# Value blocks of three attention stages one round earlier, and a projection slab in two drains

## The chip, the cores and the metric

The kernel runs on one core of a Trainium2 chip. It is written by hand, one instruction stream for each engine: TensorE (PE) for matmuls and transposes, VectorE (DVE), ScalarE (ACT), GpSimd (POOL) and SyncE (SP), which issues the loads. The engines meet only at semaphores. The metric is the device time of one execution in microseconds, as the median of some runs.

## The reference

Two blocks of a language model run one after the other on one sequence of 512 tokens with 1024 channels; all arrays are float32. The first is one layer, the second has two, so there are three attention stages, each with an input projection, an output projection and a feed-forward part.

```python
# first block: compressed, windowed and selected attention, 8 heads each, width 64
o_nsa = gates[..., 0:1] * o_cmp + gates[..., 1:2] * o_slc + gates[..., 2:3] * o_win
mixed = jnp.concatenate([o_nsa, o_swa], axis=-1) @ w_out
h = h + rms_norm(mixed, attn_post_norm)
# second block, layer 0: 8 heads of softmax attention, 8 of stick-breaking attention
o = jnp.concatenate([merge_heads(mla), merge_heads(sb)], axis=-1)
return o @ w_o
# second block, layer 1: 16 heads of softmax attention with a decay
return merge_heads(o) @ w_o
# both: x = x + mixer(norm(x)); x = x + ffn(norm(x))
```

In stick-breaking attention the weights are products of sigmoids along the keys, not a softmax.

## The kernel before

**Arithmetic.** A projection is done in three matmuls of a fast format (`mm3`, L853 to L855) on high and low halves of both operands. GpSimd splits each weight slab (128 x 1024) into `w_hi` and `w_lo` (`split_slab`, L462); the four slab rooms and the two rooms of `raw` are handed back through the semaphores `slab_used` and `split`. An output projection has two groups (c = 0 and 1, each 512 columns) of four slabs (s); a slab is four tiles (t), one for each 128 tokens, of six matmuls each, and each tile has its own PSUM bank. Slab s needs channels 256 s to 256 s + 255 of the attention's result, that is two pairs of heads, as halves `xt_hi` and `xt_lo`.

**Attention by rounds.** The stages `first` (12 pairs of heads), `mix` (8 pairs, the last 4 stick-breaking) and `fox` (8 pairs) are run by one scheme, class `Pairs` (L527). A step g is one pair and one block of 128 queries, the longest first: g modulo 4 = 0, 1, 2, 3 has 4, 3, 2, 1 blocks of keys (of `first`, the first four pairs have two at most). Every engine walks through the same rounds r in program order:

- TensorE (`pe_pair_attend`, L1215): the scores of step r; then the value blocks that `value_blocks(r)` lists (`values`, L1255, matmuls at L1266, into bank 6); then it turns the probabilities of step r-2 with transposes (L1239) into banks 4 and 5, in some rounds with the inverses of a pair's sums (L1251); then what the stage's hooks add.
- VectorE (`dve_pair_attend`, L2381): the maxima of step r, or for stick-breaking the scan along the keys (`products`, L2404); copies of the turned probabilities into `p_turn` (L2426) and of the inverses into `inv_t` (L2433); `scaled` (L2448), which reads bank 6 and multiplies by the inverses; for stick-breaking `low` (L2458).
- ScalarE (`act_pair_attend`, L1857): the exponentials (L1868) or sigmoids (L1872), its part of the copies (L1879, L1881, L1888), `high` (L1896), and hooks.
- GpSimd (`pool_first`, `pool_pairs`): widens the inverses (L674), splits the first slabs of the coming projection in the middle of the stage, and splits a pair's result into halves (`halves`, L676).

The scores go round among five banks (in `first` up to step 31 among four); those of a step wait until the exponentials of earlier steps on the same banks are done. Banks 4 and 5 hold one step's turned probabilities, so the next turning waits for both copies of the one before. Bank 6 holds one pair's output: `values` with block 0 waits until `scaled` or `low` of the pair before has read it.

**When.** For pair p the value blocks stood in rounds 4p+8 (block 0), 4p+9 (1) and 4p+10 (2 and 3), for the last pair all in 4p+8. `scaled` came in round 4p+11 (the last pair 4p+9), as did `high` and `low` of stick-breaking, and GpSimd's and ScalarE's work on a pair is placed by `scaled_round` too. After the last scores a stage has eight to ten further rounds, its drain; then comes the output projection (`pe_out_direct`, L1083, for `mix` and `fox`), slab by slab. The drain of `first` already holds two slabs of its projection by hooks (L1443 to L1446). `first` also finishes the input projection's last turnings in hooks of its early rounds; one of them, `window_there`, waits for a copy out of bank 6.

## Time and profile before

| | us |
|---|---|
| median of three runs | 1941.33 |
| lowest and highest of them | 1937.68, 1943.10 |
| the profiled execution's own time | 1936.56 |
| its span, first to last instruction | 1934.8 |
| mean granted clock of TensorE | 0.994 |
| attention of `first` | about 131 to 285 |
| attention of `mix`, its projection | about 797 to 884.5, to 928 |
| attention of `fox`, its projection | about 1444 to 1524.7, to 1568 |

The profile page gives each engine's busy time and the chain of work that ended last. The other views are windows (busy time of each engine in a stretch, with the granted clock as a share of 2.4 GHz), waits (for whom an engine stood still, in total, how often, the longest) and instructions in order of time. Busy time of matmuls overlaps with the next matmul's start, so a single duration is longer than the step from one to the next.

### The profile page before, as it was taken

The numbers are of one execution on the slowest core, as the hardware profiler recorded it, in microseconds if no ns is written. First come the engines' busy times: TensorE is split into PE (matmuls) and PEld (weight loads), VectorE is DVE, ScalarE is ACT, GpSimd is POOL, SyncE is SP. The second block draws the span as 40 slices with busy tenths as digits, with TensorE's granted clock in tenths as the row PEclk, the third lists the DMA queues.
The fourth block names the chain that finished last, engine by engine and source line by source line (L and its number), as shares of the span: only waits on it lengthen the run. The fifth ranks groups of instructions, "written<-read, shape, count | busy, mean of one in ns | idle before, by whom it ended". The sixth has DMA issues, their size and how long they took to land.

```text
span 1934.8 us, 28081 instructions
## 1 busy us (share of the span) xinstructions
PE 1865.5 (96%) x10416; PEld 1500.4 (78%) x10416; DVE 807.2 (42%) x1286; ACT 469.6 (24%) x1145; POOL 1081.9 (56%) x713
## 2 busy tenths in 40 slices
PE   8989899999999999989999999999998999999999
PEld 7776578888888887747888888887875688888887
DVE  4646756765670146671323321114527333223200
ACT  2136533222220144462211110112326221111100
POOL 6754244766666555233566666656534456666663
PEclk9999999999999999999999999999999999999999
DMA  4330022323333232201233332323211123323332
GB/s 158 105 96 13 2 77 66 105 91 98 108 98 98 74 95 69 66 23 55 88 98 96 93 95 91 104 67 98 88 55 45 32 89 98 93 93 97 98 98 87
DMA packets 122557, 159.50 MB, mean 82 GB/s; under 512 B 8546, under 2 KB 83810, under 8 KB 122465
## 3 DMA queue, kind: packets, MB, share of 16 engines
q1 hardware_dynamic: 122465, 158.21, 26.6%
q8 instruction: 65, 1.06, 0.2%
q14 instruction: 27, 0.22, 0.0%
HBM read 155.04 MB, written 2.10 MB: 81 GB/s over the span
## 4 chain that ended last, share of the span: by engine, by line
PE 89%; DVE 6%; ACT 3%; issue 1%; DMA 0%; SPq 0%; DVEq 0%; ACTq 0%
PE ps L853 25%; PE ps L855 25%; PE ps L854 25%; PE ps L1266 3%; PE ps L1239 2%; PE ps L863 1%; DVE p_turn L2426 1%; PE ps L1314 1%; PE ps L1330 1%; DVE gains L2506 1%; PE ps L1041 1%; ACT dump L1613 1%; PE ps L1344 1%; ACT tok L1868 0%; DMA h<-in_x 0%
## 5 line engine op out<-in xcount | busy, mean ns | idle before, releaser
L471 POOL TENSOR_TENSOR w_lo<-raw,w_hi 128x1024 fp32r<-128x1024 f32 (+1 forms) x256 | 605.4, 2365 | 21.4
L469 POOL TENSOR_SCALAR w_hi<-raw 128x1024 fp32r<-128x1024 f32 (+1 forms) x256 | 270.1, 1055 | 502.2 <-PE ps L855 470.6
L853 PE MATMUL ps<-xt_hi,w_hi 128*128 128x512 f32 (+2 forms) x1096 | 420.3, 383 | 0.9 <-ACT tok L2042 0.9
L855 PE MATMUL ps<-xt_hi,w_lo 128*128 128x512 f32 (+2 forms) x1096 | 419.7, 383 | 0.0
L854 PE MATMUL ps<-xt_lo,w_hi 128*128 128x512 f32 (+2 forms) x1096 | 419.6, 383 | 0.0
L853 PE MATMUL ps<-w_hi,xt_hi 128*128 128x512 f32 (+3 forms) x672 | 258.9, 385 | 8.2 <-DVE tok L2541 4.5
L855 PE MATMUL ps<-w_hi,xt_lo 128*128 128x512 f32 (+3 forms) x672 | 254.8, 379 | 0.0
L854 PE MATMUL ps<-w_lo,xt_hi 128*128 128x512 f32 (+3 forms) x672 | 254.8, 379 | 0.0
L2227 DVE TENSOR_TENSOR ps<-ps,gains 128x512 f32<-128x512 f32 x132 | 92.1, 698 | 373.6 <-PE ps L855 373.6
L853 PEld LDWEIGHTS ps<-xt_hi,w_hi 128*128 128x128 f32 (+1 forms) x1096 | 205.2, 187 | 42.3 <-POOL w_lo L485 1.3
L854 PEld LDWEIGHTS ps<-xt_lo,w_hi 128*128 128x128 f32 (+1 forms) x1096 | 205.2, 187 | 40.9
L855 PEld LDWEIGHTS ps<-xt_hi,w_lo 128*128 128x128 f32 (+1 forms) x1096 | 205.2, 187 | 40.9
L853 PE MATMUL ps<-w_hi,hid_hi 128*128 128x512 f32 x528 | 205.6, 389 | 0.0
L855 PE MATMUL ps<-w_hi,hid_lo 128*128 128x512 f32 x528 | 205.4, 389 | 0.0
L854 PE MATMUL ps<-w_lo,hid_hi 128*128 128x512 f32 x528 | 205.4, 389 | 0.0
L853 PEld LDWEIGHTS ps<-w_hi,xt_hi 128*128 128x128 f32 x672 | 127.0, 189 | 34.8 <-issue 6.0
L855 PEld LDWEIGHTS ps<-w_hi,xt_lo 128*128 128x128 f32 x672 | 126.8, 189 | 23.3
L854 PEld LDWEIGHTS ps<-w_lo,xt_hi 128*128 128x128 f32 x672 | 127.1, 189 | 21.5
L2154 DVE TENSOR_TENSOR h<-ps,h 128x512 f32<-128x512 f32 x32 | 22.0, 692 | 253.6 <-PE ps L855 253.6
L853 PEld LDWEIGHTS ps<-w_hi,hid_hi 128*128 128x128 f32 x528 | 99.1, 188 | 20.6
L854 PEld LDWEIGHTS ps<-w_lo,hid_hi 128*128 128x128 f32 x528 | 99.1, 188 | 20.6
L855 PEld LDWEIGHTS ps<-w_hi,hid_lo 128*128 128x128 f32 x528 | 99.1, 188 | 20.5
(324 smaller groups left out, 2195.7 us busy)
## 6 DMA issues: line engine op xcount, KB each, us to landing
raw<-in_w_up SPq DMA_DIRECT2D x88, 256.0 KB
raw<-in_l_w_gate SPq DMA_DIRECT2D x88, 256.0 KB
raw<-in_l_w_up SPq DMA_DIRECT2D x88, 256.0 KB
raw<-in_l_w_down SPq DMA_DIRECT2D x40, 512.0 KB
raw<-in_l_w_in SPq DMA_DIRECT2D x36, 512.0 KB
raw<-in_w_down SPq DMA_DIRECT2D x20, 512.0 KB
raw<-in_l_w_o SPq DMA_DIRECT2D x16, 512.0 KB
raw<-in_w_in SPq DMA_DIRECT2D x12, 512.0 KB
```

Source lines behind the costliest of these rows:

```text
L469: e.tensor_scalar(w_hi[:, s, 0:width], r, 1.0, 0.0, ALU.mult, ALU.add).then_inc(split, 1)
L471: e.tensor_tensor(w_lo[:, s, 0:width], r, w_hi[:, s, 0:width].bitcast(F32), ALU.subtract).then_inc(split, 1)
L853: e.matmul(o, s_hi, m_hi, start=start, stop=False)
L854: e.matmul(o, s_hi, m_lo, start=False, stop=False)
L855: return e.matmul(o, s_lo, m_hi, start=False, stop=stop)
L863: m = e.transpose(bank(turn_bank(name, i), P, t * P, w), staged(name, c)[:, t, off:off + w], ident[:, :])
L1041: m = e.transpose(bank(BY_COLUMNS[name][k], P, t * P), h[:, t, k * P:(k + 1) * P], ident[:, :])
L1239: m = e.transpose(bank(4 + y, HD, (2 * kb + x) * HD), st.prob(g, x)[r, kb * P:(kb + 1) * P], ident[r, r])
L1266: m = e.matmul(ps[x * HD:(x + 1) * HD, 6 * W + kb * P:6 * W + (kb + n) * P], value(p, x, kb), st.rooms["p_turn"][:, p % 2, x, 4 * kb:4 * k ...
L1314: e.matmul(bank(b[x], n), qp[r, q, i * P:(i + 1) * P], kk[r, k, k0 * P:(i + 1) * P], start=True, stop=False)
L2154: e.tensor_tensor(h[:, t, cs], out_half(name, c, t), h[:, t, cs], ALU.add).then_inc(*od.done(*at(f"{name}_res", NT * c + t + 1)))
L2227: e.tensor_tensor(b, b, rs_rows, ALU.mult).then_inc(*od.done(*at(f"{name}_r", 4 * gi + (j + 1))))
```

## The change

Value blocks, `scaled`, and `high` and `low` of stick-breaking stand in earlier rounds: block 0 in 4p+7, block 1 in 4p+8, blocks 2 and 3 in 4p+9, `scaled`, `high` and `low` in 4p+9; the last pair has all of its in 4p+7. A new `split_round` holds the old round numbers for GpSimd's and ScalarE's work behind `scaled`, so that its place in their orders stays. The hook `window_there` goes from round 7 to round 6. And the tiles of slab 0 of group 0 of the second and third output projection are issued by hooks in the drain: tile 0 behind round 32, tile 1 behind 33, tiles 2 and 3 behind 34, each with waits for the exponentials that used its bank; `pe_out_direct` begins with slab 1.

```diff
--- before.py
+++ after.py
@@ -549,7 +549,10 @@
             return band_prob_at(g, x) if g < 4 * self.banded else prob_at(g, x)
 
         def scaled_round(self, p):
-            return max(self.values_round(p) + 1, self.inverse_round(p) + 1)
+            return max(self.values_round(p), self.inverse_round(p))
+
+        def split_round(self, p):
+            return 4 * p + (11 if p < self.pairs - 1 else 9)
 
         def is_soft(self, g):
             return g < 4 * self.soft
@@ -565,16 +568,16 @@
             out = []
             for p in range(self.pairs):
                 if p == self.pairs - 1:
-                    rounds = {4 * p + 8: (0, 2, 1, 3) if p < self.banded else (0, 1, 2, 3)}
+                    rounds = {4 * p + 7: (0, 2, 1, 3) if p < self.banded else (0, 1, 2, 3)}
                 elif p < self.banded:
-                    rounds = {4 * p + 8: (0, 2), 4 * p + 9: (1,), 4 * p + 10: (3,)}
+                    rounds = {4 * p + 7: (0, 2), 4 * p + 8: (1,), 4 * p + 9: (3,)}
                 else:
-                    rounds = {4 * p + 8: (0,), 4 * p + 9: (1,), 4 * p + 10: (2, 3)}
+                    rounds = {4 * p + 7: (0,), 4 * p + 8: (1,), 4 * p + 9: (2, 3)}
                 out += [(p, kb) for kb in rounds.get(r, ())]
             return out
 
         def values_round(self, p):
-            return 4 * p + (8 if p == self.pairs - 1 else 10)
+            return 4 * p + (7 if p == self.pairs - 1 else 9)
 
         def inverse_round(self, p):
             return self.turn_round(4 * p + 7) if p + 1 < self.pairs else 4 * p + 6
@@ -657,9 +660,9 @@
             if r in slabs:
                 split_slab(e, *slabs[r], SLAB)
             for p in range(12):
-                if 4 <= p < 11 and r == first.scaled_round(p) + 1:
+                if 4 <= p < 11 and r == first.split_round(p) + 1:
                     added(p)
-                if ends(p) and r == first.scaled_round(p) + (1 if p < 4 or p == 11 else 2):
+                if ends(p) and r == first.split_round(p) + (1 if p < 4 or p == 11 else 2):
                     squared(p)
 
     def pool_pairs(e, st, slabs, steps=None, value_step=None):
@@ -690,7 +693,7 @@
             if steps and r in steps:
                 value_step(steps[r])
             for p in range(st.soft):
-                if r == st.scaled_round(p) + 1:
+                if r == st.split_round(p) + 1:
                     halves(p)
 
     @block.gpsimd
@@ -1080,16 +1083,32 @@
                     if norm and s - s0 == 2:
                         pe_turn_pair(e, norm, 0)
 
+    def out_tile(e, name, there, c, s, t):
+
+        if t == 0:
+            e.wait_ge(split, 2 * (4 * (phases[name].g0 + c) + s) + 2)
+            if c == 0:
+                e.wait_ge(*there[s])
+        m = slab_tile(e, name, c, s, OUT_KTS[s], x_model, KD - 1, t)
+        if t == 3:
+            m.then_inc(slab_used, 1)
+
+    def out_drain(e, name, there, probs, last):
+
+        def first_tiles(a, b, p):
+            e.wait_ge(*at(probs, p))
+            for t in range(a, b):
+                out_tile(e, name, there, 0, 0, t)
+
+        return {last + 1: lambda: first_tiles(0, 1, 2 * last), last + 2: lambda: first_tiles(1, 2, 2 * last),
+                last + 3: lambda: first_tiles(2, 4, 2 * last + 2)}
+
     def pe_out_direct(e, name, there, norm):
 
         for c in range(2):
             for s in range(4):
-                e.wait_ge(split, 2 * (4 * (phases[name].g0 + c) + s) + 2)
-                if c == 0:
-                    e.wait_ge(*there[s])
-                for t in range(NT):
-                    m = slab_tile(e, name, c, s, OUT_KTS[s], x_model, KD - 1, t)
-                m.then_inc(slab_used, 1)
+                for t in range(NT) if c or s else ():
+                    out_tile(e, name, there, c, s, t)
                 if c == 1 and s == 1:
                     pe_turn_columns(e, norm, 0)
 
@@ -1430,9 +1449,8 @@
 
         def scores_second():
             scores(1)
-            window_there()
-
-        hooks = {1: banks_there, 3: window_first, 5: scores_first, 7: scores_second, 11: lambda: turned(0),
+
+        hooks = {1: banks_there, 3: window_first, 5: scores_first, 6: window_there, 7: scores_second, 11: lambda: turned(0),
                  13: lambda: turned(1)}
         for k in range(4):
             hooks[15 + 2 * k] = lambda k=k: values(k)
@@ -1546,11 +1564,12 @@
                    lambda c: [at("in2_copy", 4 * c + 4)]
                    + ([at("in2_tok", 4 if c == CQ else 4 * HEAD_CHUNKS[c] + 8)] if c == CQ or c in HEAD_CHUNKS else []),
                    "n5")
+        mixed_halves = [at("mix_lo", 2), at("mix_lo", 4), at("mix_slo", 2), at("mix_slo", 4)]
         heads_of = lambda v: lambda p, x, kb: v[:, kb, (2 * p + x) * HD:(2 * p + x + 1) * HD]
         pe_pair_attend(e, mix, mix_scores, heads_of(v2), [at("in2_tpa", 6), at("in2_tpd", 9), at("in2_copy", 31)],
-                       [at("in2_copy", 32), at("in2_tpa", 12), at("in2_tpd", 15)])
-        pe_out_direct(e, "out2", [at("mix_lo", 2), at("mix_lo", 4), at("mix_slo", 2), at("mix_slo", 4)],
-                      "n6")
+                       [at("in2_copy", 32), at("in2_tpa", 12), at("in2_tpd", 15)],
+                       out_drain(e, "out2", mixed_halves, "mix_p", mix.steps - 1))
+        pe_out_direct(e, "out2", mixed_halves, "n6")
         pe_up(e, "up2", "n6")
         pe_down(e, "down2", "up2", "n7")
 
@@ -1589,10 +1608,11 @@
                    lambda c: ([at("in3_copy", 4 * wide("in3", c) + 4), at("in3_tok", 4 * FOX_CHUNKS[c] + 4)]
                               if c in FOX_CHUNKS else []),
                    "n7", {(2, 0): turn_logits, (2, 1): decays, (2, 2): turn_decays, (2, 3): turn_first})
+        fox_halves = [at("fox_lo", 2 * s + 2) for s in range(4)]
         pe_pair_attend(e, fox, fox_scores, heads_of(v3),
                        [at("in3_tpa", 8), at("in3_tpd", 8), at("picks", 6), at("fox_ck", 1)],
-                       [at("in3_copy", 24)])
-        pe_out_direct(e, "out3", [at("fox_lo", 2 * s + 2) for s in range(4)], "n8")
+                       [at("in3_copy", 24)], out_drain(e, "out3", fox_halves, "fox_p", fox.steps - 1))
+        pe_out_direct(e, "out3", fox_halves, "n8")
         pe_up(e, "up3", "n8")
         pe_down(e, "down3", "up3", None)
 
@@ -1820,7 +1840,7 @@
         for k in range(4):
             hooks[16 + 2 * k] = [lambda e, od, k=k: outputs(e, od, k)]
         for p in ENDS:
-            r = first.scaled_round(p) + (1 if p < 4 or p == 11 else 2)
+            r = first.split_round(p) + (1 if p < 4 or p == 11 else 2)
             hooks.setdefault(r, []).append(lambda e, od, p=p: high(e, od, p))
         return layer, hooks
 
@@ -1909,7 +1929,7 @@
             for hook in hooks.get(r, ()) if hooks else ():
                 hook(e, od)
             for p in range(st.soft, st.pairs):
-                if r == st.values_round(p) + 1:
+                if r == st.values_round(p):
                     high(p)
         if st.soft < st.pairs:
             e.preload_act_table_set(EXP_LN)
@@ -2328,7 +2348,7 @@
                  11: [lambda e, od: weights(e, od, 1)], 29: [lambda e, od: variance(e, od, 0)],
                  31: [lambda e, od: dve_refine(e, od, "first", 1, NT, 16)]}
         for p in ENDS:
-            hooks.setdefault(first.scaled_round(p) + (2 if p < 4 or p == 11 else 3), []).append(
+            hooks.setdefault(first.split_round(p) + (2 if p < 4 or p == 11 else 3), []).append(
                 lambda e, od, p=p: low(e, od, p))
         return hooks, variance
 
@@ -2472,7 +2492,7 @@
                 if r == st.scaled_round(p):
                     scaled(p)
             for p in range(st.soft, st.pairs):
-                if r == st.values_round(p) + 1:
+                if r == st.values_round(p):
                     low(p)
             for hook in hooks.get(r, ()) if hooks else ():
                 hook(e, od)
```

## Rows read from the trace of the kernel before

**Rows 1.** The page: busy time of the engines, and the chain that ended last.

```profile
PE 1865.5 (96%) x10416; PEld 1500.4 (78%) x10416; DVE 807.2 (42%) x1286; ACT 469.6 (24%) x1145; POOL 1081.9 (56%) x713
...
PE 89%; DVE 6%; ACT 3%; issue 1%; DMA 0%; SPq 0%; DVEq 0%; ACTq 0%
```

**Rows 2.** Windows: span, then busy us of PE, PEld, DVE, ACT, POOL, clock, DMA.

```profile
130.00:285.00 155.00, 138.87 (x1463) 95.02 (x1463) 104.50 (x219) 81.13 (x278) 52.76 (x46) 0.98 0.09 27
...
834.10:884.50 50.40, 37.65 (x421) 20.92 (x417) 33.39 (x48) 28.57 (x76) 7.21 (x8) 0.97 0.04 12
884.50:906.30 21.80, 21.80 (x98) 18.05 (x97) 2.77 (x4) 3.64 (x7) 10.31 (x6) 1.00 0.16 49
```

**Rows 3.** Waits of PE, 1444 to 1535: us in total, times, longest.

```profile
PE ps L1266 <- DVE o_sb L2448: 5.8, 7, 1.8
PE ps L1239 <- DVE p_turn L2426: 2.9, 7, 0.5
```

**Rows 4.** Waits of PE, 130 to 285.

```profile
PE ps L1239 <- DVE p_turn L2426: 3.6, 8, 0.8
PE ps L1266 <- DVE gains L2448: 3.5, 5, 0.9
...
PE ps L1239 <- ACT p_turn L1879: 1.0, 2, 0.5
...
PE ps L1266 <- DVE mixed L2448: 0.4, 1, 0.4
```

**Rows 5.** Waits of PE, 797 to 885.

```profile
PE ps L1266 <- DVE xt_lo L2458: 5.0, 3, 2.3
PE ps L1239 <- ACT p_turn L1881: 3.5, 4, 0.9
PE ps L1239 <- DVE p_turn L2426: 1.9, 1, 1.9
PE ps L1239 <- DVE inv_t L2433: 1.5, 1, 1.5
```

**Rows 6.** PE in order of time, 1505 to 1525: start, us, instructions, [idle before].

```profile
1505.24 1.08 PE L1266 MATMUL ps<-p_turn,v 128*64 128x512 f32 x4 [0.56 <-DVE o_sb L2448]
...
1511.99 0.28 PE L1239 MATMUL ps<-ident,tok 64*128 64x64 f32 x2 [0.39 <-DVE p_turn L2426]
...
1514.38 1.97 PE L1266 MATMUL ps<-p_turn,v 128*64 128x512 f32 x4 [1.80 <-DVE o_sb L2448]
...
1522.37 2.38 PE L1266 MATMUL ps<-p_turn,v 128*64 128x512 f32 x16 [1.21 <-DVE o_sb L2448]
1524.67 0.50 PE L853 MATMUL ps<-w_hi,xt_hi 128*128 128x512 f32 x1
```

**Rows 7.** Windows behind two waits of PE.

```profile
1514.38:1520.70 6.32, 6.32 (x37) 2.59 (x38) 1.38 (x4) 0.55 (x2) 2.44 (x3) 0.50 0.01 1
...
841.10:845.10 4.00, 3.96 (x44) 2.81 (x46) 3.40 (x6) 1.21 (x4) 1.11 (x1) 0.57 0.02 4
```

**Rows 8.** PE in order of time, at 877.

```profile
877.25 1.08 PE L1266 MATMUL ps<-p_turn,v 128*64 128x512 f32 x4 [2.27 <-DVE xt_lo L2458]
```

**Rows 9.** DVE and ACT in order of time, at 1509 to 1513.

```profile
1512.62 1.02 DVE L2426 COPY p_turn<-ps 128x384 f32<-128x384 f32 x2 [0.40 <-PE ps L1239]
...
1509.48 0.58 ACT L1868 ACTIVATE tok<-ps,nmax 128x384 f32<-128x384 f32 x1
```

**Rows 10.** PE and ACT in order of time, at 150 to 152.

```profile
150.44 0.53 PE L1312 MATMUL ps<-smalls,first_row 64*128 64x1 f32 x4
...
151.98 0.60 ACT L1700 ACTIVATE kk<-ps 128x512 f32<-128x512 f32 x1
```

**Rows 11.** DVE and POOL in order of time, at 858 to 870.

```profile
858.85 4.20 DVE L2404 TENSOR_TENSOR_SCAN tok<-tok,one 128x512 f32<-128x512 f32 x3 [0.90 <-ACT tok L1872]
...
867.50 2.33 DVE L2404 TENSOR_TENSOR_SCAN tok<-tok,one 128x512 f32<-128x512 f32 x2
...
858.74 1.27 POOL L681 TENSOR_TENSOR xt_lo<-o_sb,xt_hi 128x512 fp32r<-128x512 f32 x1
```

## The prediction

> **What bounds the kernel now.** I read the page's busy shares and its chain first: TensorE is busy for 96% of the span and the chain that ends last is TensorE for 89% [rows 1]. So only time in which TensorE stands still, or runs at half clock, can be won. Next come the windows of the three attention stages [rows 2]: the first has 155.0 - 138.9 = 16.1 us without a matmul, the second's stick-breaking half 50.40 - 37.65 = 12.8 us. In the output projection behind (884.5 to 906.3) it never stands still. Then the waits of TensorE in these stages [rows 3 to 5]: nearly all are of two kinds. A value block (L1266) waits until bank 6 has been read (`scaled`, `low`); and a turning (L1239) waits until the turned rows before it have been copied out of banks 4 and 5. At last the third stage in order of time [rows 6]: per pair of heads (9.14 us from 1505.24 to 1514.38) there is one wait of 0.56 and one of 0.39 us, and behind the last scores come 1.80 and 1.21 us.
>
> The clock is the third loss. After the 1.80 us without work TensorE was granted 0.50 of its clock, which is the 1.2 GHz level, for 1514.38 to 1520.70; after a wait of 1.9 us [rows 5] the mean was 0.57 for 4 us [rows 7]. At half clock 6.3 us of TensorE work costs about 3.2 us, and the 4 us stretch some 1.7 us. A wait of 2.27 us at 877.25 was not followed by such a stretch: the same four matmuls took 1.08 us, not the 1.97 us of 1514.38 [rows 6, 8]. So the loss is not certain for any one wait.
>
> **1. Value blocks one round earlier (all three stages).** Nothing is added. Before, rounds with number 0, 1, 2 modulo 4 had the blocks 0, 1 and 2+3, and round 3 had only one short score and a turning of three key blocks, which must wait until the turned four key blocks of round 2 are copied: that is the 0.39 us wait (1511.99). After, round 3 has block 0, 1.0 us of matmul, ahead of that turning, and round 2 has none. 1.0 us covers 0.39 to 0.5 us. Block 0 itself needs bank 6 free. Before, `scaled` for the pair before sat one round ahead in VectorE's order; now it sits in round 4p+9, two rounds ahead of block 0 of pair p+1 (4p+11): the 0.56 us goes. In the third stage that is 5 x 0.56 + 6 x 0.39 = 5.2 us [rows 3, 6].
>
> What comes next there. VectorE must now do 0.68 us of `scaled` right behind the last blocks, ahead of the maxima of the two-block score: these, the copy and so the turning of round 3 come some 0.6 us later. I count TensorE's own work from that point as 0.55 + 0.6 + 1.0 us and VectorE's as 0.7 + 0.6 us with 0.3 us to wake: the turning would be about 0.1 us short. And the score of round 3 now starts 0.8 us sooner, while its bank is freed by the first exponential of the score two rounds before, which ended at 1509.48 + 0.58 = 1510.06 [rows 9], 0.9 us ahead of that score: 0.1 us or nothing is missing. I take 0.2 us per pair (bounds 0 and 0.9): 5.2 - 1.1 = 4.1 us.
>
> **2. The end of the third stage.** Moved: the first slab of the projection, 24 matmuls, a quarter of the 21.8 us of [rows 2] over four slabs = 5.45 us, one tile 1.36 us. The work stays; it now lies in the empty rounds. Its weights were split in the stage's middle, the first two pairs are long done, banks 0 to 3 are freed by the exponentials. From 1511.99 to the end of that slab (1524.67 + 5.45) there are 18.1 us. Of these go 1.80 (block 0 of pair 6 is already done behind an earlier `scaled`), 1.21 (before the last values now lie three tiles, 4.1 us, against `scaled` and copies of 1.4 us), and the half clock, 3.2 us. New: the turning of score 30 waits for both copies of score 29 on VectorE (1.02 us, [rows 9]); only 0.8 us of blocks lie between: 0.7 us. Gain 1.80 + 1.21 + 3.2 - 0.7 = 5.5 us. Third stage: 4.1 + 5.5 = **9.6 us**, bounds 6 and 11. Other queues: the slab's release comes some 5 to 8 us earlier, so GpSimd's next split and SyncE's next load start earlier; they were waiting for it and collide with nothing but the last halves, which have 10.9 us of matmul (slabs 1 and 2) as cover before slab 3 needs them.
>
> **3. The second stage.** The waits of [rows 5] all lie in its second half; the soft half gains nothing. In the second half all waits and the half clock sum to 12.8 + 1.7 = 14.5 us [rows 2, 5, 7]. Going through it round by round: (a) the 1.9 us wait on `p_turn` ends when VectorE has done the first scan behind ScalarE's table load; block 0 has moved ahead, so this and a 0.8 us wait for bank 6 ahead of it become one wait of about 2.3 us, and the half clock stays (I keep 1.7 us). (b) 0.88 us per pair, four times [rows 5], is covered by block 0. (c) The 1.5 us wait behind `inv_t` stays (1.6 us), as it is VectorE's two rounds of scans. (d) block 0 of pairs 5 and 6 now waits for `low` behind the scans of round 1. That chain is, as an estimate from [rows 8, 11], score 1.2, sigmoid 0.9, scans 2.3 and 1.9, `low` 0.7, block 0 1.0, turning and wakings 0.8: 8.8 us a pair against 37.65 / 5 = 7.5 us of TensorE's work, so 1.35 us each in place of two of the three waits on `xt_lo` and the 0.88s. (e) In the drain the third of them (1.5 us) goes, as in part 2; 0.45 us remains. Left: 2.3 + 1.7 + 0.3 + 1.6 + 2.7 + 0.45 = 9.0 us. Gain **5.5 us**, bounds 3.5 (a half-clock stretch of 6.8 us instead of 3.4) and 7.2 (none).
>
> **4. The first stage.** It already has parts of its projection in its last rounds; only part 1 counts. Waits on bank 6: 3.5 + 0.4 = 3.9 us; on turned rows some 3.3 us of the 3.6 + 1.0 (the longest, 0.8 us, is VectorE's own norm work and stays, and 0.5 us lie ahead of the first value block) [rows 4]. Residue 1.5 us, as `high` and `low` add work in every second pair. Up to round 31 only four banks go round, so the score of round 3 needs the second exponential too: 1.0 us for the four pairs. And **a wait is added**: `window_there` moves from round 7 to round 6, as round 7 now writes bank 6. It waits for ScalarE's copy of the last window key, which ended at 151.98 + 0.60 = 152.58; TensorE began round 7 at 150.44 [rows 10]. Queued behind it are the scores, values and turning of round 7; ScalarE and VectorE then wait for these. 2.3 us of wait, of which 0.7 us was half clock anyway: 1.7 us (bounds 1.0 and 3.4, if the clock stays low). Gain 7.2 - 1.5 - 1.0 - 1.7 = **3.0 us**, bounds -1 and 5.
>
> **A rule to weigh.** In the second stage three scans over 512 and 384 columns took 4.20 us while GpSimd split a pair (858.74), and two over 512 took 2.33 us without it [rows 11]: about 1.0 us lost, in three pairs. The splits' rounds are unchanged but their input comes two rounds sooner, so they slide from the long scans to the short ones two rounds earlier. The Trainium skill (SBUF — State Buffer, "Who interferes with whom") says that a VectorE instruction with two SBUF inputs contends with a GpSimd one that reads SBUF and that the second to issue waits for the whole of the first. The trace agrees in size. In my sum the slide is free, since the short scans' results are asked for two rounds later.
>
> **Sum.** 9.6 + 5.5 + 3.0 = 18.1 us. The profiled execution took 1936.56 us (span 1934.8): 1918.5. The three timed runs have a median of 1941.33, 4.8 us above it; the same subtraction gives **1923**.
>
> **Rivals.** (A) *VectorE takes TensorE's place.* For: in the second half of stage two it already sets the pace; if `scaled` in the crowded round costs its full 0.68 us in each of some 15 pairs, 10 us go. Against: it is busy for 104.5 of 155 us in stage one and 33.4 of 50.4 in stage two's half [rows 2]. Gain 8: 1933. (B) *The port.* By the rule above the splits now stop the short scans; if these are then late for `low`, 1.0 us in three pairs: gain 15, 1926. (C) *It does not do what it says:* block 0 and the tiles wait on something else in program order, so that only the drains' clock moves: gain 3, 1938. (D) *Slower.* The bank of round 3's score: it starts 0.8 us sooner, but the exponential that frees it follows a ScalarE copy which itself waits for TensorE's turning. If it came 1.4 us late, not 0.1, each of 24 pairs would pay 1.3 us more, 31 us against 18: 1954. It decides from 0.75 us per pair on. Against it stand the 0.9 us that the first exponential had in hand.
>
> **How the numbers follow.** Forecast 0.68, A 0.17, B 0.05, C 0.06, D 0.04. Range: the forecast's own bounds (all lows 8.5, all highs 23) and most of A and B: 1915 to 1934. What a measurement of this kernel can tell from no change is about 0.3%, 5.8 us: faster 0.90 (forecast, A, B), the same 0.06 (C), slower 0.04 (D).
>
> **What would show it.** Third stage: waits of L1266 on `o_sb` gone, the period 8.3 to 8.5 us instead of 9.14, no half-clock stretch, projection matmuls between values 6 and 7. First stage: a new TensorE wait of about 2.3 us ahead of round 7, ended by L1702/L1700 of ScalarE. Second stage: the wait at the table load still there. Wrong if the scores' lines wait on L1868, if turnings wait on VectorE for over 0.3 us per pair, or if new half-clock stretches appear.

## The result, and the profile after

Lines of kernel.py after the change: `mm3` L856 to L858, turning L1258, inverses L1270, `values` L1285, the scores' first matmuls L1331 to L1363, `scaled` L2468, `low` L2478, scans L2424.

| | before | after |
|---|---|---|
| median, us | 1941.57 (4 runs) | 1918.78 (4 runs) |
| lowest and highest | 1937.68, 1943.10 | 1915.74, 1923.58 |
| profiled execution, and its span | 1936.56, 1934.8 | 1915.74, 1914.0 |
| mean granted clock in it | 0.994 | 0.992 |

The ratio is 0.9888, with a 95% interval of 0.9860 to 0.9916. A later series on another occasion gave 1921.18 (6 runs) against 1942.17 (17 runs), ratio 0.9897 (0.9879 to 0.9916). The forecast of 1923 us, 18.1 us saved, stands against 20.8 us between the two profiled executions and 21.0 to 22.8 us between the medians.

I measured the stages between fixed marks: a stage's first score, the first score of stick-breaking, and a turning behind the output projection. Savings in us:

| stretch | forecast | measured |
|---|---|---|
| ahead of the first stage | 0 | 1.9 |
| first stage | 3.0 | 1.5 |
| second stage, soft half, and the work ahead of it | 0 | -1.1 |
| second stage, stick-breaking half and drain | 5.5 | 8.4 |
| third stage and drain | 9.6 | 10.0 |
| everything else | 0 | 0.1 |

The 1.9 us ahead of the first stage lie in the kernel's first matmuls, which the change doesn't touch: the second group of 16 transposes of the input took 3.67 us in before (at 10.33) and 1.97 us in after (at 10.79), and the first matmuls of the projection behind it took up to 0.78 us in before and 0.48 in after. It is clock, and in this execution it fell to after. The same marks in the later execution `after_again`: 0.6, -6.4, -0.6, 9.8 and 10.0 us. The third stage repeats; the second moves by 1.4 us and the first by nearly 8 with the clock, on which more below.

The page of after, busy time and the chain, against [rows 1]: TensorE's share rises by one point because the span shrinks; its work doesn't.

```profile
PE 1864.6 (97%) x10416; PEld 1499.7 (78%) x10416; DVE 801.9 (42%) x1286; ACT 468.9 (25%) x1145; POOL 1084.0 (57%) x713
...
PE 89%; DVE 6%; ACT 3%; issue 1%; DMA 0%; SPq 0%; DVEq 0%; ACTq 0%
```

Windows of after, against [rows 2]: span, busy us of PE, PEld, DVE, ACT, POOL, granted clock, DMA. The first is the first stage, the second the stick-breaking half with its drain up to just ahead of the last values, the third these values and the projection behind them, without a pause.

```profile
128.10:283.10 155.00, 143.66 (x1469) 98.09 (x1470) 101.59 (x219) 81.61 (x278) 55.63 (x46) 0.94 0.10 29
831.80:875.70 43.90, 38.55 (x419) 22.59 (x416) 32.05 (x46) 27.24 (x72) 8.29 (x8) 0.96 0.05 13
875.70:897.50 21.80, 21.80 (x102) 16.95 (x101) 3.46 (x5) 4.78 (x10) 11.66 (x8) 1.00 0.23 72
```

In the stick-breaking half TensorE now stands still for 43.90 - 38.55 = 5.35 us, where it was 12.8. In the first stage its busy time rose by 4.8 us and the granted clock is 0.94 instead of 0.98. Of the 4.8 us 1.5 are work behind the stage, which is shorter by that much; the other 3.3 are half clock, which took part of what the waits gave back.

Waits of PE in the third stage of after, 1433.2 to 1524, against [rows 3] (total, times, longest). There is no row for L1285 left; the two turnings on `p_turn` are 0.53 us at the stage's start, as in before, and 0.41 us at its end. The waits on the exponentials (`tok`) at the stage's start are of before as well.

```profile
PE ps L1363 <- ACT tok L1888: 1.2, 1, 1.2
PE ps L1258 <- DVE p_turn L2446: 0.9, 2, 0.5
PE ps L1258 <- ACT tok L1888: 0.8, 1, 0.8
```

PE in order of time at the end of the third stage of after, against [rows 6]: start, us, instructions, idle before. The first row is block 0 of pair 5, the second that of pair 6 (in before at 1505.24 and 1514.38).

```profile
1487.72 1.08 PE L1285 MATMUL ps<-p_turn,v 128*64 128x512 f32 x4
...
1495.99 1.08 PE L1285 MATMUL ps<-p_turn,v 128*64 128x512 f32 x4
...
1498.80 0.46 PE L1258 MATMUL ps<-ident,tok 64*128 64x64 f32 x8 [0.41 <-DVE p_turn L2446]
1499.19 0.50 PE L856 MATMUL ps<-w_hi,xt_hi 128*128 128x512 f32 x1
...
1500.77 0.87 PE L1285 MATMUL ps<-p_turn,v 128*64 128x256 f32 x8
...
1507.01 2.37 PE L1285 MATMUL ps<-p_turn,v 128*64 128x512 f32 x16
1509.31 0.50 PE L856 MATMUL ps<-w_hi,xt_hi 128*128 128x512 f32 x1
```

A pair takes 8.27 us instead of 9.14. Block 0 of pair 6 takes 1.08 us at full clock, where the 1.80 us wait had left it 1.97 us at half clock. The tiles lie where the two waits were, and the last values (1507.01) start without one.

Waits of PE in the second stage of after, 794 to 876, against [rows 5]. The waits on `xt_lo` fell from 5.0 to 1.3 us and the four on ScalarE's `p_turn` from 3.5 to 0.3; the pair around the table load (`p_turn` 1.28 and `inv_t` 1.04) and the one behind `inv_t` (1.44) remain.

```profile
PE ps L1258 <- DVE inv_t L2453: 2.5, 2, 1.4
PE ps L1258 <- DVE p_turn L2446: 1.3, 1, 1.3
PE ps L1285 <- DVE xt_lo L2478: 1.3, 2, 0.6
...
PE ps L1258 <- ACT p_turn L1901: 0.3, 1, 0.3
```

Waits of PE in the first stage of after, 128 to 283, against [rows 4], and under them the same engine in order of time. The waits on bank 6 are gone. 0.25 us in five pairs now waits for the copy of the inverses (`gains` L2453). The window wait ahead of round 7 is there, 1.97 us.

```profile
PE ps L1331 <- ACT kk L1720: 2.0, 1, 2.0
...
PE ps L1406 <- ACT vbd L1833: 1.3, 1, 1.3
...
PE ps L1258 <- DVE gains L2453: 1.3, 5, 0.3
...
PE ps L1258 <- DVE p_turn L2446: 0.7, 2, 0.4
```
```profile
144.53 2.21 PE L1406 MATMUL ps<-kct,qp 128*128 128x64 f32 x16 [1.35 <-ACT vbd L1833]
...
152.00 0.59 PE L1331 MATMUL ps<-smalls,first_row 64*128 64x1 f32 x4 [1.97 <-ACT kk L1720]
```

### The profile page after: what moved, and what is told of

It reads as the page before. It is cut to its first block, busy times and chain, and to the rows that moved or that the text cites. A ratio compares the mean times of both kernels' runs of the same rounds, so it can differ in the third digit from the quotient of the medians.

```text
span 1914.0 us, 28081 instructions
## 1 busy us (share of the span) xinstructions
PE 1864.6 (97%) x10416; PEld 1499.7 (78%) x10416; DVE 801.9 (42%) x1286; ACT 468.9 (25%) x1145; POOL 1084.0 (57%) x713
## 4 chain that ended last, share of the span: by engine, by line
PE 89%; DVE 6%; ACT 3%; issue 1%; DMA 0%; SPq 0%; DVEq 0%; ACTq 0%
PE ps L856 26%; PE ps L858 26%; PE ps L857 26%; PE ps L1285 3%; PE ps L1258 2%; PE ps L866 1%; PE ps L1363 1%; PE ps L1333 1%; PE ps L1349 1%; DVE gains L2526 1%; ACT tok L1888 1%; PE ps L1044 1%; DVE tok L2424 1%; DVE ps L2553 0%; DVE nmax L2412 0%
## 5 line engine op out<-in xcount | busy, mean ns | idle before, releaser
L856 PE MATMUL ps<-xt_hi,w_hi 128*128 128x512 f32 (+2 forms) x1096 | 420.9, 384 | 0.9 <-ACT tok L2062 0.9
L858 PE MATMUL ps<-xt_hi,w_lo 128*128 128x512 f32 (+2 forms) x1096 | 420.3, 384 | 0.0
L856 PE MATMUL ps<-w_hi,xt_hi 128*128 128x512 f32 (+3 forms) x672 | 259.5, 386 | 7.6 <-DVE tok L2561 4.5
L858 PE MATMUL ps<-w_hi,xt_lo 128*128 128x512 f32 (+3 forms) x672 | 255.6, 380 | 0.0
L856 PEld LDWEIGHTS ps<-xt_hi,w_hi 128*128 128x128 f32 (+1 forms) x1096 | 205.4, 187 | 42.2 <-POOL w_lo L485 1.3
L858 PEld LDWEIGHTS ps<-xt_hi,w_lo 128*128 128x128 f32 (+1 forms) x1096 | 205.4, 187 | 40.7
L856 PE MATMUL ps<-w_hi,hid_hi 128*128 128x512 f32 x528 | 205.9, 390 | 0.0
L858 PE MATMUL ps<-w_hi,hid_lo 128*128 128x512 f32 x528 | 205.7, 390 | 0.0
L856 PEld LDWEIGHTS ps<-w_hi,xt_hi 128*128 128x128 f32 x672 | 127.2, 189 | 33.8 <-issue 6.0
L858 PEld LDWEIGHTS ps<-w_hi,xt_lo 128*128 128x128 f32 x672 | 127.0, 189 | 23.2
L856 PEld LDWEIGHTS ps<-w_hi,hid_hi 128*128 128x128 f32 x528 | 99.2, 188 | 20.6
L858 PEld LDWEIGHTS ps<-w_hi,hid_lo 128*128 128x128 f32 x528 | 99.2, 188 | 20.4
```

Of the source, the lines that this page charges most:

```text
L856: e.matmul(o, s_hi, m_hi, start=start, stop=False)
L858: return e.matmul(o, s_lo, m_hi, start=False, stop=stop)
```

## The experiments

Each ran beside the kernel before on one chip, in three series (medians of before: 1943.67, 1942.25 and 1942.17 us, 17 runs each). Besides times I compare **time times mean granted clock**, as an estimate of the time at full clock: an execution at 1940 us and 0.990 is 1920.6. The clock is known to 0.001, so one value is good to 1 to 2 us, and time spent waiting is counted a little low. For before the mean is 1921.3, 1922.0 and 1920.9 us in the three series, for after 1900.7 (10 runs). In these kernels a line can stand up to four further down or one further up than in after (in `before_cat`, one further up than in before).

**One part alone.** `a_only` has the value blocks and no tiles in the drains; `pe_out_direct` issues the first slab as before.

```diff
-                       [at("in2_copy", 32), at("in2_tpa", 12), at("in2_tpd", 15)],
-                       out_drain(e, "out2", mixed_halves, "mix_p", mix.steps - 1))
+                       [at("in2_copy", 32), at("in2_tpa", 12), at("in2_tpd", 15)])
...
-                for t in range(NT) if c or s else ():
+                for t in range(NT):
```

> Value blocks, scaled, high and low in their new rounds in all three stages, but no projection tiles in the drains (slab 0 comes behind the attention as before). My theory: the value blocks win the waits between rounds and the half clock at the end of the third stage, the tiles only cover the short waits of the two drains, about 3 us in each. So 14 to 16 us faster than the kernel before, the second and third stage each some 3 us longer than with the whole change; the drain waits between values of pair 6 and of pair 7 show up on L1270's and L1285's lines. Rival (the tiles are the main part in the drains): only 8 to 10 us faster. Rival (the tiles do nothing): 20 to 22 us faster.

Measured: 1923.56 us (6 runs), ratio 0.9900 (0.9881 to 0.9918), 20 us faster and not 14 to 16. In the third stage 9.05 us were saved instead of 9.99, in the second 6.69 instead of 8.40. So the tiles are worth 0.9 + 1.7 us, less than I thought (in the second stage a wait of 1.84 us ahead of the last values, which the tiles cover). The value blocks' order alone removes the 1.80 us wait and, with it, the half clock of 1514.38. In the third stage this takes the place of the 1.21 us wait:

```profile
PE ps L1270 <- POOL inv_w L677: 1.2, 1, 1.2
```

`b_only` has the tiles and all value blocks in their old rounds (`value_blocks(r)` asks for r - 1, `values_round` and `scaled_round` are one more, `window_there` is back in round 7).

> Only the projection tiles in the drains; value blocks, scaled, high and low in the rounds of the kernel before, the window wait in round 7 as before. My theory: only the waits ahead of the last pair's values (1.21 us in the third stage, 1.51 us in the second) are covered, as those ahead of pair 6's block 0 (1.80 and 2.27 us) lie before the first tile; the half-clock stretch of 6.8 us at the end of the third stage stays: 2.5 to 4 us faster than the kernel before. Rival (tiles are the main part): 8 us or more. With a_only the sum would be 17 to 19 us, less than the whole, since the tiles cover the 0.7 us waits only once the blocks have moved.

Measured: 1940.00 us (12 runs), ratio 0.9983 (0.9969 to 0.9996): 3 to 4 us, as expected. Third stage 3.4 us saved, second 0.7. Waits of PE in its third stage, 1440 to 1535: all on `o_sb` remain but one, and the largest of before, 1.8 us, is still there; the 1.21 us ahead of the last values is gone. Behind the 1.8 us no half clock followed in this execution, which is the larger part of the 3.4 us; the wait itself was not touched, and whether the tiles behind it or chance kept the clock up, this run doesn't tell.

```profile
PE ps L1288 <- DVE o_sb L2472: 4.6, 6, 1.8
PE ps L1261 <- DVE p_turn L2450: 2.9, 7, 0.5
```

At full clock the parts add: 18.5 us for the value blocks (1902.8) and 1.6 us for the tiles (1919.7) are 20.1 us, against 20.6 for both.

**Where `scaled` stands.** `scaled_late` leaves everything and puts `scaled` of the soft pairs back by one round, from 4p+9 to 4p+10; the block 0 that needs its bank is in 4p+11.

```diff
-            return max(self.values_round(p), self.inverse_round(p))
+            return max(self.values_round(p), self.inverse_round(p)) + 1
```

> The whole change, but scaled one round later for every pair: round 4p+10 in place of 4p+9, so one round ahead of the next pair's block 0 in place of two, and out of the round that also holds the maxima of three blocks and two copies. Theory (VectorE has room, what is left per pair is its order): in the third stage the 0.14 us wait on inv_t per pair goes or turns into one on o_sb ahead of block 0 (4p+11) of up to 0.5 us; the period of 8.26 us moves by less than 0.4 us, the whole time by less than 6 us, more likely slower. Rival A of the prediction (VectorE is crowded in round 4p+9): the kernel becomes 3 us or more faster than the whole change.

Measured: 1943.63 us (10 runs), ratio 1.0004 (0.9989 to 1.0018). The whole gain is gone, where I had expected less than 6 us of difference and less than 0.4 us in the period, which rose from 8.27 to 9.36 us. Its third stage, waits of PE from 1444 to 1535 and one of them in order of time:

```profile
PE ps L1288 <- DVE o_sb L2471: 6.2, 6, 1.0
```
```profile
1478.15 1.08 PE L1288 MATMUL ps<-p_turn,v 128*64 128x512 f32 x4 [1.03 <-DVE o_sb L2471]
```

The third stage saves 3.4 us instead of 10.0. At full clock (1917.6 against 1900.7 of after) one round costs 17 us, and 4 of the 21 us are left; the rest of the loss is clock. Its half-clock stretch of 37.5 us in the first stage is no longer than that of `after_again`, against whose profiled execution it is 21.6 us slower. So VectorE is not crowded by the early `scaled` (rival A); what carries the gain is that `scaled` now runs two rounds ahead of the block that waits for it.

**The second stage: GpSimd beside the scans.** `halves_held` keeps the splits of the second stage's results back until the scores of step 4p+12, near where they ran in before.

```diff
             e.wait_ge(*at(f"{name}_x", p + 1))
+            if name == "mix":
+                e.wait_ge(*at("mix_s", 4 * p + 13))
```

> The whole change, but in the second stage GpSimd's split of a pair also waits for the scores of step 4p+12, so that it falls on the long scans as in the kernel before. Rival B of the prediction, and the page's rule on the shared port: the first 512-column scan beside it again takes 2.0 to 2.2 us in place of 1.2, in two or three rounds, and the stick-breaking half becomes 1 to 3 us longer. If the scans have slack or the collision is not what made them long: scans of 1.2 us or no change of the stage's length within 0.3 us.

Measured: 1924.57 us (4 runs), ratio 0.9918 (0.9893 to 0.9943). The second stage saves 5.08 us instead of 8.40. DVE and POOL in order of time, first in `halves_held`, then in after:

```profile
851.15 4.22 DVE L2426 TENSOR_TENSOR_SCAN tok<-tok,one 128x512 f32<-128x512 f32 x3 [2.87 <-ACT tok L1894]
...
851.35 2.09 POOL L686 TENSOR_TENSOR xt_lo<-o_sb,xt_hi 128x512 fp32r<-128x512 f32 x1
```
```profile
850.44 2.97 DVE L2424 TENSOR_TENSOR_SCAN tok<-tok,one 128x256 f32<-128x256 f32 x3
...
854.11 3.19 DVE L2424 TENSOR_TENSOR_SCAN tok<-tok,one 128x512 f32<-128x512 f32 x3 [0.38 <-ACT tok L1892]
...
851.62 1.51 POOL L684 TENSOR_TENSOR xt_lo<-o_sb,xt_hi 128x512 fp32r<-128x512 f32 x1
```

Beside a split the three long scans take 4.22 us, without one 3.19. Taken singly, the first scan in `halves_held` (851.15, 1.22 us) is undisturbed, the split that starts 0.2 us behind it takes 2.09 us instead of 1.27, and the second scan, which starts while the split still runs, takes 2.23 us instead of 1.20:

```profile
851.15 1.22 DVE L2426 TENSOR_TENSOR_SCAN tok<-tok,one 128x512 f32<-128x512 f32 x1 [2.87 <-ACT tok L1894]
...
852.29 2.23 DVE L2426 TENSOR_TENSOR_SCAN tok<-tok,one 128x512 f32<-128x512 f32 x1
```

In after the splits (850.61 to 853.13) lie beside the short scans, which lengthen too (2.97 us for three that take 1.58 alone, at 858.64), but nobody waits for those. TensorE's waits in `halves_held` show it: at the table load 2.4 instead of 1.28 us, behind `inv_t` 2.5 instead of 1.44, and on one of the two blocks behind `low` 1.27 instead of 0.63. By the Trainium skill (SBUF — State Buffer, "Who interferes with whom") such a pair contends and the second to issue waits for the whole of the first. The trace agrees, in size too: the split ends at 853.44, 1.07 us behind the end of the first scan (852.37), near the 1.27 us that it takes alone, and the second scan ends at 854.52, 1.08 us behind the split, near its 1.20. In before the split was first (858.74, 1.27 us), and the scan that started 0.11 us behind it took 2.24 us.

**The second stage: the table load.** `turn_first` lets VectorE copy the turned rows of steps 14 and 15 ahead of its first scans.

```diff
+            early = 4 * st.soft <= r < min(st.steps, 4 * st.soft + 2)
+            for g in st.turned_in(r) if early else ():
+                turned(g)
...
-            for g in st.turned_in(r):
+            for g in () if early else st.turned_in(r):
                 turned(g)
```

> The whole change, but in rounds 16 and 17 of the second stage VectorE copies the turned probabilities of the last soft steps before its first scans, not behind them. Theory (the wait of 1.28 us at the change to stick-breaking comes from VectorE's order behind ScalarE's table load): it goes, with most of the 1.04 us behind it, and the scans of step 16 start as early as before: 1.5 to 2.3 us faster in the profile at the same clock, and the half-clock stretch of 3.4 us that followed is likely gone (another 1.7 us). Rival (the table load itself is what everybody waits for): the waits only move to the turnings of steps 16 and 17, less than 0.5 us won.

Measured: 1922.98 us (6 runs), ratio 0.9908 (0.9889 to 0.9926). This theory failed: the waits of 1.28 and 1.04 us became one of 3.10 us behind `inv_t`, and the stage saved 7.56 us instead of 8.40. VectorE's first scans are themselves what TensorE waits for; putting something ahead of them only moves the wait. Waits of PE, 794 to 860:

```profile
PE ps L1258 <- DVE inv_t L2453: 4.5, 2, 3.1
```

**The first stage.** `first_old` leaves the first stage as in before (as `b_only`, for `first` alone); `p0_old` does so for its first pair only, which brings the window wait back to round 7.

```diff
+        def late(self, p):
+            return int(self.name == "first" and p == 0)
...
-                out += [(p, kb) for kb in rounds.get(r, ())]
+                out += [(p, kb) for kb in rounds.get(r - self.late(p), ())]
...
-
-        hooks = {1: banks_there, 3: window_first, 5: scores_first, 6: window_there, 7: scores_second, 11: lambda: turned(0),
+            window_there()
+
+        hooks = {1: banks_there, 3: window_first, 5: scores_first, 7: scores_second, 11: lambda: turned(0),
```

> The whole change in the second and third stage, the first stage as in the kernel before (window wait in round 7). My theory from the two traces: in the first stage the change takes away 6.5 us of waits between rounds, of which 2.0 us come back as the wait ahead of round 7, and its half-clock stretches grow from 6.8 to 17.1 us, which costs about 5 us: net 1.5 us won. So 19 to 21 us faster than the kernel before, 1 to 2 us slower than the whole change, and half clock in the first stage 6.8 us again. Rival (the longer half clock has nothing to do with the change but is chance): half clock in the first stage is again long, 17 us, and this kernel is 5 us slower than the whole change.

> The whole change but for the first pair of the first stage: its value blocks are in rounds 8 to 10 and its scaled in round 10, so that the window wait is again in round 7. Theory A (the 2.0 us wait ahead of round 7 prolongs the half clock): the wait is gone, half clock in the first stage 6.8 us, 6 to 8 us faster than the whole change, 27 to 29 us faster than the kernel before. Theory B (the half clock comes from the wait for ScalarE's second layer at 144.5 and where it falls; the wait of round 7 is innocent): half clock about 17 us as with the whole change, only 2 us faster than it.

Measured: `first_old` 1923.13 us (6 runs), ratio 0.9891 (0.9869 to 0.9913); time times clock 1908.4, against 1900.7 of after: at full clock the first stage's part is worth nearly 8 us, but the times differ by only 2 to 4. My expectation of 6.8 us at half clock failed: its first stage, with the waits of before and no window wait, ran 17.1 us at half clock behind the same 1.93 us wait at the compressed scores that was followed by 6.8 us in before, and TensorE was busy all through:

```profile
144.40:161.50 17.10, 17.10 (x119) 14.07 (x120) 4.88 (x11) 4.86 (x20) 4.41 (x3) 0.50 0.11 32
```

`p0_old` 1913.12 us (5 runs), ratio 0.9847 (0.9826 to 0.9869), 1900.5 at full clock, so no work was saved against after, only clock. Its 1.97 us wait was gone, a new one of 1.05 us (values behind `scaled`) came, and the profiled execution, the slowest of the five, still had 27.3 us at half clock. They began at 135.0, 8 us ahead of the 1.1 us wait at the compressed scores. That the window wait alone holds the clock down (theory A of the expectation) has fallen with this, and theory B with the time: it is 6 to 8 us below after and not 2. The times improved, but the profiled execution shows a long stretch without that wait.

**The early waits and the clock.** In after, two waits stand close together: 1.35 us ahead of the compressed scores in round 5, for `vbd`, which ScalarE copies late, and the window's 1.97 us. `cat_later` puts the first half of the compressed scores into round 6, ahead of the window wait: `vbd` has a round more, and 16 matmuls (2.0 us) now lie ahead of the wait for the copy of the window key. So it takes from both waits at once.

```diff
         def scores_first():
             scores(0)
-            window_key(1)
+            window_there()
...
-        hooks = {1: banks_there, 3: window_first, 5: scores_first, 6: window_there, 7: scores_second, 11: lambda: turned(0),
+        hooks = {1: banks_there, 3: window_first, 5: lambda: window_key(1), 6: scores_first, 7: scores_second, 11: lambda: turned(0),
```

> The whole change, but the first half of the compressed scores moves from the hook of round 5 to that of round 6 of the first stage, ahead of the window wait; the transposes of the window key stay in round 5. At full clock this covers up to 1.3 us of the wait for ScalarE's second layer and 1.4 us of the 2.0 us wait ahead of round 7. Theory C (these two waits, close together, are what keeps the first stage at half clock for 10 to 27 us in one execution and 7 in another): half clock after 140 us falls to 7 us or less in the profile, the granted clock of the timed runs rises from 0.990 to 0.993 or more, and the median is 6 to 10 us below that of the whole change. Rival (the half clock has another cause, as the many short transposes): clock as before, 2 to 3 us faster.

Measured: **1906.73 us** (5 runs, 1905.31 to 1908.27), ratio 0.9827 (0.9806 to 0.9848), 12 to 14 us below after. Its waits of PE, 136 to 160, and then the same 11 us (146 to 157) as windows of after and of `cat_later` (the seventh figure is the clock):

```profile
PE ps L866 <- ACT kk L1720: 0.8, 1, 0.8
...
PE ps L1331 <- ACT kk L1720: 0.2, 1, 0.2
```
```profile
146.00:157.00 11.00, 9.03 (x69) 6.65 (x68) 3.16 (x6) 2.87 (x11) 4.41 (x3) 0.53 0.01 1
```
```profile
146.00:157.00 11.00, 10.52 (x145) 8.08 (x146) 7.26 (x15) 5.02 (x19) 6.01 (x5) 1.00 0.17 51
```

In the same 11 us TensorE issued 145 matmuls instead of 69 (part of that is work: `cat_later` is some rounds further on by then). The only half clock of this first stage lies earlier, from 130.0 to 136.8, ahead of round 5; from there to 175 it is full. Time times clock is 1900.6, within 0.1 us that of after, so nearly all of the 12 us is clock. An effect of the waits, or of chance? The last series put this to the test, with the same edit on the kernel before, both edits on after, and after itself once more.

> The kernel before with one edit: the scores against the selected block (half 0) stand in the hook of round 6 instead of round 5; the copy of the window key stays in 5 and its wait in 7. In the profiled run of before, the scores of round 5 waited 1.9 us for ScalarE's vbd; the window wait is not there. Theory C (two waits of nearly 2 us close together in the early rounds decide how long the first stage runs at half clock): before has only one of the two, so the edit takes 1 to 1.9 us of wait away and makes half clock in the first stage short (7 us or none instead of 7 to 17): 3 to 7 us faster, mean clock 0.993 to 0.996, time times clock within 1 us of before less the wait. Rival (the place of the half-clock stretches is chance and cat_later only drew a good one): time and clock as before within 2 us.

> The kernel after with both edits: the first pair of the first stage in its old rounds with the window wait back in round 7 (p0_old, 5.7 us faster than after), and the scores against the selected block in round 6 (cat_later, 12 us faster). Theory C: both act on the same thing, the half clock behind the early waits, so they don't add: 1904 to 1909 us, mean clock 0.996 to 0.997, time times clock 1900.5. Rival (each takes its own wait away, and they add): 1899 to 1903 us.

> The kernel after, word for word, beside the two others on one chip. If the time of after is steady: 1917 to 1921 us at a mean clock of 0.989 to 0.992, time times clock 1900.5. Theory C expects its half clock in the first stage again to be 13 us or more, and the waits of 1.3 and 2.0 us of rounds 5 and 7 both there; the rival (chance) expects a stretch that can as well be gone, and single times down to 1907.

Measured: `before_cat` 1935.96 us (12 runs, one of them an outlier at 4763 us that ratio and clock leave out), ratio 0.9966 (0.9954 to 0.9978); the 1.9 us wait is gone, one of 0.8 us came, time times clock is 1922.3 and so not lower than before: the 6.2 us are clock (0.9934 against 0.9894). `cat_p0` 1908.19 us (6 runs), ratio 0.9846 (0.9817 to 0.9874), no better than `cat_later`: the two edits act on the same loss. Five of its executions took 1906.45 to 1909.41 us, the sixth 1922.34 at a clock of 0.986, with nothing in the record to say where its half clock lay. `after_again` 1921.18 us (6 runs, 1918.70 to 1923.22), as steady as the first time. No execution of after, of ten, came near the 1907 us of `cat_later`. Its profiled execution has this window:

```profile
137.00:175.00 38.00, 34.77 (x272) 26.78 (x272) 15.45 (x39) 13.94 (x53) 7.73 (x7) 0.51 0.05 15
```

The same program that had 17.1 us at half clock in this part in one execution has 37.5 us in another, with nearly the same waits (1.12 and 1.97 us, where after had 1.35 and 1.97). And the two waits did not start it. In `after_again` they end at 146.07 and 155.01, and half clock began at 136.9. In after they end at 144.53 and 152.00, and there are two stretches, one ahead of both and one from between them on:

```profile
136.00:142.80 6.80, 6.80 (x65) 5.34 (x62) 3.43 (x11) 2.78 (x13) 0.61 (x1) 0.50 0.00 0
142.80:146.20 3.40, 2.05 (x27) 1.92 (x23) 1.54 (x5) 2.55 (x11) 0.00 (x0) 1.00 0.00 0
146.20:156.40 10.20, 8.23 (x62) 5.85 (x61) 3.13 (x6) 2.27 (x8) 4.18 (x3) 0.50 0.01 2
```

At the stage's start every kernel has a wait of 1.8 us at its first score, and most have one of 1.2 and one of 0.4 us soon behind. The edit of `cat_later` leaves these where they are; it takes away the part of the half clock that lies behind round 5.

## Why the prediction was right

**Third stage, 9.6 forecast, 10.0 measured.** Of part 1, up to the stage's last score (1510.99 and 1495.42, from the first at 1445.05 and 1434.22), I forecast 4.1 us; it is 65.94 - 61.20 = 4.7. Of the end I forecast 5.5; it is the rest, 5.3. The period was 8.27 us (8.3 to 8.5 forecast), the new wait on the turning of score 30 is 0.41 us (0.7), and the half-clock stretch is gone. In all eight profiles that share this stage's code (after twice, `first_old`, `p0_old`, `halves_held`, `turn_first`, `cat_later`, `cat_p0`) the saving is 10.0. How much half clock it takes away depends on the execution of before that it is measured against: with the same 1.80 us wait, `before_cat` had two stretches of 3.4 us there and `b_only` none. Part 2 counted the 1.80 us and the half clock among what the drain gives; `a_only` shows that the order of the value blocks alone brings both, and that the tiles bring 0.9 us.

**Second stage, 5.5 forecast, 8.4 measured (7.8 with the 0.6 us that the soft half lost).** (a) was right: 1.28 + 1.04 = 2.32 us around the table load, 2.3 forecast, and the 3.4 us half-clock stretch behind it stayed in this execution (0.53 from 839.0 to 842.6), though not in that of `after_again`, which saved 9.8: so it costs 1.4 us, for which I kept 1.7. (b) right. (c) 1.6 against 1.44. **The term that was mis-sized is (d)**: the chain through `low` was sized at 8.8 us a pair and is 8.06 (block 0 at 858.87 and 866.93), so that its wait is 0.63 us and not 1.35, twice (by its own terms, 8.8 - 7.5, it should have been 1.3). The scans take 3.95 us from the first one's start to `low`, instead of 2.3 + 1.9, and 0.63 us instead of 0.9 pass from the sigmoid's start to the scan; that is two thirds of the difference, the rest I did not itemise. The rule to weigh was right that the slide of the splits is free in after, but it left out what hangs on it: 3.3 us by `halves_held`. Had the splits stayed beside the long scans, the gain would have been 5.1. The sum had this in it unsaid, since (d) reckons with scans of 2.3 + 1.9 us, as they are without a split.

**First stage, 3.0 forecast, 1.5 measured.** The waits went as forecast or better: TensorE stood still for 11.3 us instead of 16.1, the window wait is 1.97 us (2.3), the residue 1.25 us (1.5), and the wait for a bank (1.0) all but absent: one of 0.2 us. That is 4.8 us less waiting, where the sum without its clock terms had 7.2 - 1.5 - 1.0 - 2.3 = 2.4. Where I was off is the clock: I charged the window wait with 1.7 us (2.3 - 0.7, which is 1.6), and with up to 3.4 if the clock stays low, and in this execution 17.1 us at half clock stood against 6.8 in before. 10.2 us more, in part waits, cost 3.3 us of busy time: 4.8 - 3.3 = 1.5, which is what was measured. In `after_again`, with 37.5 us at half clock, the same stage is 6.4 us longer than in before, below the forecast's bound of -1. At full clock the part is worth nearly 8 us (`first_old`).

**The total** is near the forecast by luck as well as by reckoning. The third stage is right in its parts. In the second and first the waits shrank by more than forecast, and in the first the clock took most of that back. Another 1.9 us came from the clock ahead of the first stage, which no term had. The executions with a long stretch of half clock, such as that of `after_again` (1923.22 us), are as much this kernel as the one of 1915.74. And the medians put the saving near the forecast's upper bounds: all of them together gave 23 us, which is 1918 from the median of before and not the 1915 of the range, and 21.0 to 22.8 were measured.

**The rivals.** A (VectorE crowded) and C (does not do what it says) are refuted by the traces above. D (a late bank in round 3, 1.3 us a pair) too: no score in the third stage waits behind the first 1.2 us, and one in the first stage waits 0.2 us. B had the right mechanism with the wrong sign: the split and the scans do contend, and the change moved the split to where it does no harm. In the second stage no wait shows that the short scans beside the splits are late.

## What to carry to other kernels

When one engine is nearly always busy, ask of each wait which instruction on the other engine ends it and how many rounds ahead of its reader it stands: here one round of `scaled` was worth 17 us at full clock (22 to 25 us between the medians), while filling the empty rounds with projection work brought 2.6. Where waits such as the 1.35 and 1.97 us here stand close together, try moving work into them before looking for anything finer: in this kernel that was worth 12 to 14 us, in the kernel before 6, and nearly all of it was clock. And where times move with the clock, compare time times clock over several executions, and not one profile with another. And when a step slides in time, look at what it ran beside before as well as at what it will run beside: what it leaves can be the gain.

## What the runs showed of the chip

**The clock differs from execution to execution of one program and is most of the scatter.** Over the first rounds of the first stage TensorE was granted half its clock (the 1.2 GHz level) for 6.8 us (before), 17.1 (after), 37.5 (`after_again`, `scaled_late`), 27.3 (`p0_old`, `halves_held`, `turn_first`), 27.3 (`a_only`), 23.9 (`b_only`) and 17.1 us (`first_old`), but for 3.4 to 6.8 us in `before_cat`, `cat_later` and `cat_p0`, in which the waits of rounds 5 to 7 are at most 0.8 us. Where it began differs too: in five profiles (before, `first_old`, `scaled_late`, `halves_held`, `turn_first`) within 0.8 us of the end of the 1.93 us wait for `vbd`; in after, `a_only` and `b_only` first at 131.9 to 137.2, for 3.4 to 6.8 us, and again at 145.5 to 147.4, 0.6 to 2.1 us behind the end of that wait; in `after_again` and `p0_old` at 136.9 and 135.0, without a break. In the three kernels without that wait it began at 129.6 to 136.8, ended by 140.2, and did not come again in these rounds. The times of before spread from 1934 to 1947 us; those near 1935 have a mean clock of 0.993, those near 1945 of 0.987 to 0.989. Their standard deviation is 2.9 to 3.4 us in a series, and 1.3 to 1.4 us once they are multiplied by the clock. A single profile can therefore not tell what an edit costs in clock; `p0_old` looked bad in its profile and was 5.7 us faster in its runs.

**Why the stretches differ in length stays open.** The same program had 17.1 and 37.5 us, and the same first stage with the same waits 6.8 us in before and 17.1 in `first_old`, where TensorE was busy for all of the 17.1. So the length of the waits doesn't settle it. That the edit of `cat_later` makes them short is shown: by three profiles, and by the mean clocks, 0.995 to 0.998 in ten executions of `cat_later` and `cat_p0` (the eleventh has 0.986) against 0.987 to 0.992 in ten of after. That it does so by way of the waits is argued and not shown: the edit also moves 16 matmuls of 64 columns to another round, and no run moved these without touching a wait. Nor were the two waits separated, since `p0_old` took one away and gained 6 to 8 us, and `cat_later` shortened both.

**A half clock isn't bound to the longest wait.** The 2.27 us wait at 877.25 in before was not followed by one, and the 1.26 us wait of `cat_p0` in round 8 neither; after the 1.80 us wait of the third stage there were 6.8 us in before, two stretches of 3.4 in `before_cat` and none in `b_only`.
